# The first layer's gate projection: three narrow matmuls per weight tile, or one wide and one narrow

## The reference, cut to what matters

```
h = rms_norm(x, mix_norm)
(u_a, q_b, f_b, i_b, og_b, cx_c, v_c, o_c, ig_c, fg_c, gates) = split(h @ w_in)
y_a = s5_mixer(u_a, ...)          # a complex linear recurrence
y_b = hgrn2_mixer(q_b, f_b, ...)  # gated linear attention
y_c = mlstm_mixer(cx_c, v_c, ...)
merged = sigmoid(g_a) * (y_a @ wb[:r_a]) + sigmoid(g_b) * (y_b @ wb[r_a:r_b]) + sigmoid(g_c) * (y_c @ wb[r_b:])
x = x + merged @ w_out
```

## Time and profile before

| | us |
|---|---|
| median of 3 runs | 2943.59 (2941.97 to 2943.74) |
| the profiled execution | 2942.16 |
| its span, first to last instruction | 2940.4 |
| TensorE busy | 2902.9 (99%) |
| VectorE busy | 2041.8 (69%) |
| ScalarE busy | 1311.7 (45%) |

### The profile page before, as it was taken

How to read it: one execution, slowest core, us unless ns; L and a number is a source line. 1 busy time by engine, 2 the same in 40 slices (tenths; PEclk the granted TensorE clock), 3 DMA queues, 4 the chain that set the end, 5 groups by cost and what they waited for, 6 DMA issues and landing times.

```text
span 2940.4 us, 47013 instructions
## 1 busy us (share of the span) xinstructions
PE 2902.9 (99%) x18564; PEld 2604.2 (89%) x18564; DVE 2041.8 (69%) x2634; ACT 1311.7 (45%) x1421; POOL 71.9 (2%) x72
## 2 busy tenths in 40 slices
PE   8999999999999999999999999998999999999999
PEld 8898899999988888888888888877988888888888
DVE  6674788978788888885557777638666666666444
ACT  5344524344454444444444354426344444444333
POOL 0000000000001000000000000000000000000000
PEclk9999999999999999999999999999999999999999
DMA  6553334555555555555555554531555555555555
GB/s 234 185 186 130 122 120 159 167 172 200 186 193 192 193 192 194 191 182 188 195 191 203 198 182 177 187 139 72 186 193 193 190 195 191 194 192 182 189 194 185
DMA packets 87358, 530.41 MB, mean 180 GB/s; under 512 B 9952, under 2 KB 10336, under 8 KB 41184
## 3 DMA queue, kind: packets, MB, share of 16 engines
q1 hardware_dynamic: 87264, 529.11, 51.6%
HBM read 526.97 MB, written 2.10 MB: 180 GB/s over the span
## 4 chain that ended last, share of the span: by engine, by line
PE 94%; DVE 4%; ACT 1%; issue 0%; DMA 0%; SPq 0%; DVEq 0%; ACTq 0%
PE bank L584 73%; PE late L584 21%; DVE arena L1729 1%; DVE half_low L1729 1%; DVE arena L1726 0%; DVE w_low L1729 0%; DVE xrs L1770 0%; ACT w_high L1239 0%; DVE xtmp L1729 0%; PE late L1180 0%; DMA xT<-in_xT 0%; DVE small L2589 0%; ACT arena L1700 0%; DVE acts_both L1729 0%; DVE rows_r L1726 0%
## 5 line engine op out<-in xcount | busy, mean ns | idle before, releaser
L1729 DVE TENSOR_TENSOR w_low<-ring,w_high 128x2048 fp32r<-128x2048 f32 (+1 forms) x480 | 1014.5, 2114 | 386.6 <-ACT w_high L1239 382.4
L1239 ACT ACTIVATE w_high<-ring 128x2048 fp32r<-128x2048 f32 (+1 forms) x480 | 849.7, 1771 | 629.0 <-DMA ring<-in_w_down 223.7
L584 PE MATMUL bank<-up_early,w_high 128*128 128x512 f32 x1408 | 487.8, 389 | 0.0
L584 PE MATMUL bank<-up_late,w_high 128*128 128x512 f32 x1408 | 487.4, 389 | 0.0
L584 PE MATMUL late<-acts_both,w_high 128*128 128x512 f32 x1408 | 479.0, 389 | 0.3 <-DVE w_low L1729 0.3
L584 PE MATMUL bank<-up_early,w_low 128*128 128x256 f32 x1408 | 388.9, 276 | 0.0
L584 PE MATMUL bank<-up_late,w_low 128*128 128x256 f32 x1408 | 388.9, 276 | 0.0
L584 PE MATMUL late<-acts_both,w_low 128*128 128x256 f32 x1408 | 388.8, 276 | 0.0
L584 PEld LDWEIGHTS bank<-up_early,w_high 128*128 128x128 f32 x1408 | 264.5, 188 | 55.0
L584 PEld LDWEIGHTS late<-acts_both,w_high 128*128 128x128 f32 x1408 | 264.3, 188 | 55.2 <-DVE w_low L1729 0.6
L584 PEld LDWEIGHTS bank<-up_late,w_high 128*128 128x128 f32 x1408 | 264.1, 188 | 54.9
(11 more groups left out here) (322 smaller groups left out, 4878.9 us busy)
## 6 DMA issues: line engine op xcount, KB each, us to landing
ring<-in_w_up SPq DMA_DIRECT2D x176, 1024.0 KB, 4.7
ring<-in_w_down SPq DMA_DIRECT2D x128, 704.0 KB, 4.1
ring<-in_w_in SPq DMA_DIRECT2D x66, 1024.0 KB, 4.8
ring<-in_w_mix SPq DMA_DIRECT2D x62, 1024.0 KB, 4.8
ring<-in_w_gates SPq DMA_DIRECT2D x96, 512.0 KB, 3.8
ring<-in_w_branch SPq DMA_DIRECT2D x16, 1024.0 KB, 4.7
ring<-in_w_out SPq DMA_DIRECT2D x16, 1024.0 KB, 4.7
ring<-in_w_o SPq DMA_DIRECT2D x16, 1024.0 KB, 4.8
```

The source lines that it names most:

```text
L584: return nc.tensor.matmul(o, lhsT, rhs, start=first, stop=last)
L1239: A(w_high[:, s, 0:cols], ring[:, s, 0:cols], ACT.Copy).then_inc(rounded[s], 1)
L1729: return V.tensor_tensor(o, a, b, op)
```

## The change

TensorE's unit now has, for each half, 8 matmuls of 512 columns (`half_high` against `h_high` and `h_low` side by side, into both halves of the bank) and then 8 of 256 columns (`half_low`), 32 matmuls in place of 48. The high and the low parts of `h` stay where they were; `h_both` is a view of both with a fixed step between them. The unit's result then stands in two halves of the bank, which must be added before the Sigmoid. ScalarE copies the first half into `arena` (`gate_copied`), VectorE adds the second half to it (`sum_gate`) and thereby frees the bank, and ScalarE applies Sigmoid in place, one unit later. On VectorE `sum_gate(c)` stands inside `lower_gate` of unit c+2, between its two halves; the last two sums stand behind the loop. The ring's rounded halves move by 64 bytes, and 256 bytes are left free behind the ring, by which all later buffers move.

```diff
+        sb("ring_pad", [P, 4 * HALF_SHIFT // 4])
...
-        half_high = alias("half_high", ring_base, [P, RING, HALF], 2 * UNIT // T)
+        half_high = alias("half_high", ring_base, [P, RING, HALF], 2 * UNIT // T, HALF_SHIFT)
... TensorE, gate()
-                        mm(bank[at][:, 0], half_high[:, s, c], h_high[:, k], k == 0, False)
-                        mm(bank[at][:, 0], half_high[:, s, c], h_low[:, k], False, False)
+                        mm(bank[at][:], half_high[:, s, c], h_both[:, :, k * T:(k + 1) * T], k == 0, False)
... ScalarE, gate(c)
-                at = gate_tile(c)
-                A(arena[:, at * T:(at + 1) * T], bank[s][:, 0], ACT.Sigmoid).then_inc(drained[s], 1)
+                A(gate_at(c), bank[s][:, 0], ACT.Copy).then_inc(gate_copied, 1)
+                if c:
+                    gate_sigmoid(c - 1)
+                waiting[c] = (s, halves.drained[s].value())
+            def gate_sigmoid(c):
+                s, there = waiting[c]
+                act.wait_ge(drained[s], there)
+                A(gate_at(c), gate_at(c), ACT.Sigmoid)
... ScalarE, after the last unit
             gate(GATES - 1)
+            gate_sigmoid(GATES - 1)
... VectorE
+            def sum_gate(c):
+                at = (2 * c + 1) % RING
+                dve.wait_ge(gate_copied, c + 1)
+                tt(gate_at(c), bank[at][:, 1], gate_at(c), ADD).then_inc(drained[at], 1)
             def lower_gate():
                 for half in range(2):
                     s, _, _, _, _ = half_units.next(False, split=True)
+                    if half and gates[0] >= AHEAD:
+                        sum_gate(gates[0] - AHEAD)
                     dve.wait_ge(half_rounded[s], half_units.rounded[s].value())
                     tt(half_low[:, s], half_raw[:, s], half_high[:, s].bitcast(F32), SUB).then_inc(half_lowered[s], 1)
+                gates[0] += 1
... VectorE, behind the last lower_gate, ahead of y_low
+            for c in range(GATES - AHEAD, GATES):
+                sum_gate(c)
```

More of the change, by code:

```diff
@@ L101 @@
 GATES, HALF = 48, UNIT // 2
+HALF_SHIFT = 64
 GATES_FED = 46
@@ L266, in build @@
         u_high = alias("u_high", arena_base, [P, S5_TILES, T], 127)
-        h_high, h_low = alias("h_high", arena_base, [P, KT, T], 46), alias("h_low", hT_base, [P, KT, T])
+        h_apart = (arena_base - hT_base) // 4 + 46 * T
+        h_both = alias("h_both", hT_base, [P, 2 * h_apart])[:].rearrange("p (a d) -> p a d", a=2)[:, :, 0:KT * T]
+        h_low, h_high = (h_both[:, a].rearrange("p (k t) -> p k t", t=T) for a in range(2))
         half_raw = ring[:, 0:2].rearrange("p s (q c) -> p (s q) c", c=HALF)
         half_low = alias("half_low", ring_base, [P, RING, HALF])
-        half_high = alias("half_high", ring_base, [P, RING, HALF], 2 * UNIT // T)
+        half_high = alias("half_high", ring_base, [P, RING, HALF], 2 * UNIT // T, HALF_SHIFT)
         y2_all, y2_band = alias("y2_all", arena_base, [P, HEADS, T], 0), alias("y2_band", arena_base, [P, HEADS, T], 26)
@@ L383, in build @@
         half_copied = sem("ff_low_half_copied")
+        gate_copied = sem("gate_low_half_copied")
         x_normed, gains_made = sem("x_normalised"), sem("mix2_gains_made")
@@ L404, in v, with gate_at @@
             return vec[0:rows_, c:c + 1]
+        def gate_at(c):
+            at = gate_tile(c)
+            return arena[:, at * T:(at + 1) * T]
         def all_tiles(sq, n):
@@ L1416, in gate @@
                 act.wait_ge(half_consumed[s], there)
-                at = gate_tile(c)
-                A(arena[:, at * T:(at + 1) * T], bank[s][:, 0], ACT.Sigmoid).then_inc(drained[s], 1)
+                A(gate_at(c), bank[s][:, 0], ACT.Copy).then_inc(gate_copied, 1)
+                if c:
+                    gate_sigmoid(c - 1)
+                waiting[c] = (s, halves.drained[s].value())
+            waiting = {}
+            def gate_sigmoid(c):
+                s, there = waiting[c]
+                act.wait_ge(drained[s], there)
+                A(gate_at(c), gate_at(c), ACT.Sigmoid)
             def round_gate():
@@ L1962, in _ @@
             half_units.skip(4, False)
+            gates = [0]
+            def sum_gate(c):
+                at = (2 * c + 1) % RING
+                dve.wait_ge(gate_copied, c + 1)
+                tt(gate_at(c), bank[at][:, 1], gate_at(c), ADD).then_inc(drained[at], 1)
             def lower_gate():
```

## The result

The changed kernel takes 2957.5 us (median of 5 runs, 2954.69 to 2960.84), the kernel before 2943.6 beside it (2941.36 to 2946.08). The ratio is 1.0046, with a 95% interval of 1.0035 to 1.0057, so it is slower by 10 to 17 us. The forecast was 2948.7 us, within 2940 to 2956, no change that can be told; the time lies just above that range. The execution profiled after the change has a span of 2955.8 us and a time of 2957.56; its span is 15.4 us longer than the one of before.

A forecast was written before the change was run, and what follows sets the result against it. TensorE was taken to bound the kernel overall, VectorE from 347 to 378 and 455 to 500 us. Terms summed to +3.7, plus 1.4 for the clock, +5.1: 2947.3 us, or 2948.7 against the median; range 2940 to 2956.

The forecast's parts named there:

- the clock (+1.4): Around unit 8: TensorE idle over 4 us brings one more fall of the granted clock, +1.4 us.
- Units 0 to 4: 300 to 347 us, on TensorE's path: five units each save 0.21 us, -1.05 us.
- Units 9 to 16: On TensorE's path after unit 8: eight units each save 0.21 us, -1.68 us.
- third rival: Gate units: wide matmuls 0.235 us apart as in token units, 17 units lose 0.13 each, +2.2, 2950.9 us; chance 0.12.
- 347 to 378 us and unit 8, with its clock: Two sums on VectorE's path, +0.68; unit 8 starting after subtraction and sum, +1.79; one clock fall, +1.4 us.
- 454 to 500 us: Unit 15's Sigmoid ahead of ScalarE's read of unit 16, +0.38; six sums on VectorE's path, +2.04 us.
- Three S5 rounds: From 500 us, units 24 to 44: both engines nearly full, 43.6 against 43.5 us, taken as 0; bounds -4.2 and +1.9.
- Units 45 to 47: On TensorE's path after the S5 rounds: three units each save 0.21 us, -0.63 us.
- End of the stage: Unit 47's sum delays y_low and w_low; branch matmuls start 4.0 us late, a later wait swallowed, +2.2 us remains.
- The clock rival: TensorE idle ahead of unit 8 and first branch unit: each clock fall costs 1.4, up to 2951.5 us; chance 0.30.
- holds up nothing inside the loop: VectorE's sum_gate waiting for ScalarE's copy: no cost, since unit c+2's second half, queued behind, cannot load earlier anyway.
- two signs of being wrong: Three S5 rounds well under 3 x 45 us, or the first w_low starting as soon as its rounding is done.

The follow-up runs named there:

- e7_alternate: e5_copy_both with wide and narrow matmuls alternating in each unit, in place of eight wide then eight narrow; ratio 1.0032 to the kernel before.
- e6_end_order: Changed kernel with VectorE making both y_low before the last two sums and ScalarE copying unit 47 before rounding the first branch unit; 2952.5 us, ratio 1.0032.
- e11_sum_first: Changed kernel with each sum moved ahead of the first of its unit's two subtractions, still freeing the bank; ratio 1.0012 to the kernel before.
- e4_spare_sums: Kernel before plus, in 46 units, an unused 256-column addition on VectorE between the two subtractions, nothing waiting for it; 2946.9 us, ratio 1.0015.
- e5_copy_both: Changed kernel with ScalarE copying both halves out and freeing the bank; VectorE's sum, in its old place, reads the copy; ratio 1.0014 to the kernel before.
- e9_mixed: e10_copy_both_end with pairs only in units 0 to 3, 8 to 14, 23 to 47, and the kernel before's addresses; ratio 0.9988 to the kernel before.
- e10_copy_both_end: e5_copy_both with y_low ahead of the last two sums and unit 47's copy ahead of rounding the first branch unit; ratio 0.9997 to the kernel before.

## Why the prediction was wrong

It had the direction of its sum (+3.7) and of the clock (+1.4) right, and the mechanism in one sentence: unit c+2 can start only when VectorE is through its first subtraction and the sum. The step that failed is the one after it, which priced this at unit 8 alone. The terms, with what the two traces show between the same points (TensorE's idle time from 300 to 680 us grew from 9.1 to 20.8 us, and the clock took some 4 more, 2.7 in unit 8 and up to 1.7 at the first branch matmuls):

- *Units 0 to 4: -1.05; measured -0.6. Units 9 to 16: -1.68; measured -1.0.* The size was off. Wide matmuls follow one another by 0.233 us, not 0.227, and a unit saves 0.12 to 0.14 us (from 6.00 to 5.88 beside HGRN2, from 5.92 to 5.78 beside S5), not 0.21. This is nearly the 0.235 of the third rival and of the token units; I set it aside for the feed-forward's, where the second operand is laid out as here. `e7_alternate` shows that this argument was wrong even for alternating matmuls. The warm gap of the Trainium skill (TensorE: Matmul & The Clock Gate, section "Back-to-back issue gap"), which the page gives for an isolated matmul and not for a stream of them, would by estimate have a wide one save 2.5 ns over two narrow ones. Measured it is 2 x 119.8 - 233.1 = 6.5, between that and my 13.
- *347 to 378 us and unit 8, with its clock: +0.68 + 1.79 + 1.4 = +3.9; measured +5.4, from unit 5 to unit 9.* The wait came as described, 4.18 us against "over 4". The clock behind it was lost for about twice as long as assumed: unit 8 took 2.7 us more than the next ones, not 1.4. In `e6_end_order` and `e11_sum_first` it was lost for less or not at all there, so this part varies. Unit 7 too waited for a sum (0.74 us); ahead of it I had counted the additions' own time alone.
- *454 to 500 us: +0.38 + 2.04 = +2.4; measured +3.2 to the start of unit 24.* `e4_spare_sums` puts VectorE's time at 2.0 here; units 18, 20 and 21 wait 0.5, 1.35 and 1.4 us for a sum, and no term held such waits.
- *Three S5 rounds: 0, bounds -4.2 and +1.9; measured +2.9, outside the bounds.* This is the failed step proper. I compared how much each engine has to do in a round, 43.6 against 43.5 us, and took the result as a tie. But the order on VectorE decides, not the load: the sum stands behind up to 5.8 us of other work. `e4_spare_sums` has the same load and loses nothing in these rounds; `e5_copy_both` has load and wide matmuls and gains 1.7 from unit 24 to unit 45; the change loses 2.9.
- *Units 45 to 47: -0.63; measured +0.3.* Unit 47 waited 0.45 us for a sum.
- *End of the stage: +2.2; measured +2.0* (+2.4 to the first branch matmul, less 0.4 until the output projection, where the second wait of the earlier trace rows is gone and the clock is lost once). Right in its steps (`w_low` starts 4.0 us behind its rounding, at 671.51), and `e6_end_order` confirmed the 2.4. The size is in part luck: the branch matmuls were to start 4.0 us late, but the branch unit was rounded 2.8 us after the GLU's first matmul and not 4.3 as before; and of the 1.55 us of the second wait, the fall of the clock took most back.

The clock rival, with 2951.5 us at most, came closest to the time. It named the idle time ahead of unit 8 and of the branches, and both falls came, but the greater loss is TensorE's waiting itself. The sentence that the added wait "holds up nothing inside the loop" was true of VectorE's own queue, and there I stopped: I asked who waits behind the waiting instruction and not, for every unit, who waits for the instruction. Of what the profile was to show, VectorE's 43 to 44 of 45 us came (43.9), but the three rounds did not stay "as long as before": each took 1.0 us more, and TensorE has idle time from 500 on. Neither of the two signs of being wrong that I had named came about; both looked for a kernel faster than forecast.

That the range was missed, and not only the forecast, hangs on the 2.5 us in the output projection: without them the profiled execution would have come to about 2955 us, inside it. The failed step does not hang on them.

What stays open: how much the clock's falls add on average, since single executions show them in different places; what makes the output and down projections take one of two lengths, and whether a change ahead of them makes the longer one likelier; and how much of the lead of `e9_mixed` over `e10_copy_both_end` comes from its pairing.

## What to carry to other kernels

When a bank's release moves from an engine with time to spare to one with a long queue, price it by what stands ahead of the releasing instruction in that queue at each unit, not by the instruction's own 0.34 us or by the engine's load. Let the idle engine copy the bank out and free it, or put the releasing instruction first among its neighbours: here that was worth 9 to 10 us for the copy, some 4 of them clock, and 6 to 10 for moving one line. And try the faster form only where its engine leads: the spare sums cost 2.0 us from unit 20 to unit 24, where VectorE leads, and nothing in the S5 rounds, and the one kernel with both forms came out 0.12% below the kernel before, where the one with pairs throughout came out even with it, though its addresses differ as well.

## What the hardware showed that I had not expected

- The pitch of matmuls depends on where their operands lie: `half_high` 64 bytes further on, with all buffers behind the ring 256 bytes further on, took the narrow ones from 119.8 to 117.2 ns and the wide ones from 230.4 to 233.1. Which of the two moves did it was not tried.
- The same stage with the same code runs at two pitches in the executions of different kernels at a granted clock of 1.00: the first down projection in 239.9 or 246.7 us. The rows of the output projection above show the two pitches, 0.34 and 0.35 us a pair. Each kernel was profiled once, so that one program has both pitches is not shown.
- GpSimd's additions stretched VectorE's subtractions with two operands in SBUF by 6% on average (1221 to 1297 ns): those that overlap one took 1399 ns, the others 1218. The Trainium skill (SBUF — State Buffer, section "Who interferes with whom") says that the two engines share a pair of ports under an exclusive lock, and that a VectorE instruction with two SBUF inputs contends with a GpSimd instruction that reads SBUF. The trace agrees that they disturb each other, by 76 ns an instruction on average.
